# Mixer projections: halves of them moved between other TensorE steps, and half of the weights' low parts made by GpSimd

## The reference, cut to what matters

```python
h = _rmsnorm(x, norm1_g[l])            # 256 tokens, 1024 channels
p = h @ w_in[l]                        # 1024 x 4128
(gq, gk, gv, gz, ga, gb, mq, mk, mv, mo, mi, mf) = jnp.split(p, offsets, axis=-1)
y_a = _gdn_group(gq, gk, gv, gz, ga, gb, conv_w[l], ...)   # conv, silu, l2norm of q and k, gates
y_b = _mlstm_group(mq, mk, mv, mo, mi, mf, ...)
```

## Time and profile before

| | us |
|---|---|
| median of 3 runs | 1675.83 (1675.46 to 1678.76) |
| the profiled execution | 1690.07 |
| its span | 1688.2 |
| PE busy in the span | 1483.8 |
| DVE busy | 1105.5 |
| ACT busy | 583.5 |
| POOL busy | 828.1 |

### The profile page before, as it was taken

One profiled execution on the slowest core, in us unless ns is written; L12 is line 12 of the kernel. 1 busy time (PEld: TensorE's weight loads), 2 busy tenths in 40 slices (PEclk: granted clock), 3 DMA queues, 4 the chain that ended last, 5 costly groups with the idle time before them and its releaser, 6 DMA issues.

```text
span 1688.2 us, 22193 instructions
## 1 busy us (share of the span) xinstructions
PE 1483.8 (88%) x8310; PEld 1058.9 (63%) x8310; DVE 1105.5 (65%) x2162; ACT 583.5 (35%) x847; POOL 828.1 (49%) x746
## 2 busy tenths in 40 slices
PE   8999999756666799998878875889999989999999
PEld 7997675744222366665433431438998876699987
DVE  5865633797587868786756664317886547568865
ACT  6753331211121221232000001127665454466652
POOL 0025220467777765656667767642775113027750
PEclk9999999988787799999999987999999999999999
DMA  7447860698999999999999989995555554545451
GB/s 278 150 150 317 311 233 25 256 380 307 402 406 368 378 389 402 403 404 402 399 406 405 396 322 405 383 363 190 177 175 191 182 198 201 207 143 181 173 197 50
DMA packets 154251, 477.15 MB, mean 283 GB/s; under 512 B 10016, under 2 KB 12320, under 8 KB 150944
## 3 DMA queue, kind: packets, MB, share of 16 engines
q0 software_dynamic: 73728, 268.47, 41.1%
q1 hardware_dynamic: 80416, 207.27, 33.7%
HBM read 474.65 MB, written 1.05 MB: 282 GB/s over the span
## 4 chain that ended last, share of the span: by engine, by line
PE 56%; DVE 11%; DMA 11%; POOL 9%; issue 6%; ACT 2%; another core or an unknown queue 1%; ACTq 0%; DVEq 0%; POOLq 0%
PE ps L673 55%; POOL arena L2802 8%; DMA arena<-in_peer_v,cl 6%; DMA arena<-in_peer_u,arena 3%; DVE arena L1851 3%; PE ps L677 1%; POOL wring L2802 1%; DVE arena L1466 1%; DVE arena L1472 1%; DVE wring L1851 1%; DMA wring<-in_peer_u,arena 1%; DMA wring<-in_ada 1%; DVE st L2096 0%; DVE arena L1469 0%
## 5 line engine op out<-in xcount | busy, mean ns | idle before, releaser
L673 PE MATMUL ps<-arena,wring 128*128 128x256 f32 (+2 forms) x2360 | 603.4, 493 | 115.0 <-DMA arena<-in_peer_v,cl 92.2
L673 PEld LDWEIGHTS ps<-arena,wring 128*128 128x128 f32 (+1 forms) x2360 | 330.6, 167 | 368.6 <-issue 171.5
L1851 DVE CUSTOM_DVE_ANT_0 arena<-arena 128x1024 f32<-128x1024 f32 x214 | 257.2, 1225 | 141.4 <-DMA arena<-in_peer_u,arena 88.9
L2802 POOL DMA_INDIRECT arena<-in_peer_u,arena x214 | 243.0, 1136 | 201.7 <-DVE arena L1809 77.5
L2802 POOL DMA_INDIRECT arena<-in_peer_v,cl x214 | 231.0, 1080 | 85.5 <-issue 60.7
L673 PE MATMUL ps<-hhl,wh 128*128 128x256 f32 (+1 forms) x1056 | 252.4, 322 | 1.2 <-POOL hhl L2812 0.7
L2190 ACT ACT_TABLE_LOAD x64 | 82.1, 1283 | 406.5 <-DVE arena L1851 228.3
L1466 DVE TENSOR_TENSOR wl<-wring,wh 128x2048 fp32r<-128x2048 f32 (+1 forms) x76 | 168.1, 2212 | 60.0 <-ACT wh L2193 58.1
L673 PE MATMUL ps<-hhl,wl 128*128 128x256 f32 x704 | 198.5, 282 | 0.0
L673 PEld LDWEIGHTS ps<-hhl,wh 128*128 128x128 f32 x1056 | 175.6, 190 | 19.6 <-POOL hhl L2812 2.5
L2193 ACT ACTIVATE wh<-wring 128x2048 fp32r<-128x2048 f32 (+1 forms) x78 | 146.2, 1874 | 70.8 <-PE ps L673 69.0
(11 more groups left out here) (257 smaller groups left out, 2025.3 us busy)
## 6 DMA issues: line engine op xcount, KB each, us to landing
wring<-in_ups SPq DMA_DIRECT2D x33, 2048.0 KB
wring<-in_ada SPq DMA_DIRECT2D x24, 2048.0 KB, 11.5
wring<-in_ffn_w_down SPq DMA_DIRECT2D x12, 2048.0 KB
wring<-in_w_in SPq DMA_DIRECT2D x8, 2048.0 KB
wring<-in_ffn_w_down SPq DMA_DIRECT2D x6, 1536.0 KB
wring<-in_peer_wq SPq DMA_DIRECT2D x4, 2048.0 KB
wring<-in_attn_w_qkv SPq DMA_DIRECT2D x4, 2048.0 KB
wring<-in_w_out SPq DMA_DIRECT2D x2, 2048.0 KB
```

Of the source, the lines that this page charges most:

```text
L673: return pe.matmul(o, l, r, start=start, stop=stop)
L1851: ve.tensor_tensor_reduce(out=o, in0=o, in1=h2[:, t, :], scale=1.0, scalar=0.0, op0=MUL, op1=ADD, accum_out=dots[j % 2][:, k:k + 1]).then_ ...
L2802: po.indirect_dma_start(out=ring[n % NR], out_offset=None, in_=table, in_offset=bass.IndirectOffsetOnAxis(ap=which, axis=0)).then_inc(S[f" ...
```

## The change

Three things move. PE does the first half of projection 1 where six `busy` matmuls stood, ahead of `crow`, and the first half of projection 6 ahead of the l2 sums of q, whose five `busy` matmuls are taken out. The low parts of pieces 1, 3, 5, 7, 9 and 11 go from DVE to POOL, on a counter of their own, `g_wl`. And DVE's `lo_in(2)` stands ahead of the copy of `crow` instead of behind the negated maxima.

```diff
-        "v_gu": ("v_gps", 1), "v_ge": ("v_gu", 1), "v_gl": ("v_ge", 1), "v_wl": ("v_hT", 4), "a_wh": ("a_hTh", 1), "v_cum": ("v_gl", 1), "v_cc": ("v_cum", 1),
+        "g_lev": ("g_wl", 6), "v_gu": ("v_gps", 1), "v_ge": ("v_gu", 1), "v_gl": ("v_ge", 1), "v_wl": ("v_hT", 4), "a_wh": ("a_hTh", 1), "v_cum": ("v_gl", 1), "v_cc": ("v_cum", 1),
...
+    def low_there(p):
+
+        return ("g_wl", p // 2 + 1) if p % 2 == 1 and p < 12 else ("v_wl", p // 2 + 1 + p // 13)
...
-        def proj3(n):
+        def proj3(n, halves):
...
-            for g in range(2):
+            for g in halves:
                 b = take(("pj", 2 * n + g), "a_pj", 2 * n + g + 1)
                 for i in range(2):
                     p = 2 * n - 2 + (i if n == 3 else g)
-                    pe.wait_ge(*at("v_wl", p + 1))
+                    pe.wait_ge(*at(*low_there(p)))
...
         k.then_inc(S["p_cum"], 1)
-        busy(bank_ada[:, 0:128], 6)
+        proj(1, [0])
         pe.wait_ge(*at("v_cc", 1))
         b = take("crow", "v_crow", 1)
...
         def l2(g, n):
-            busy(bank_ada[:, 0:128], 5 * n)
             pe.wait_ge(*at("a_l2s", n + 1))
...
-        proj(1)
+        proj(1, [1])
         pe.wait_ge(*at("v_rows", 1))
...
         proj(5)
+        proj(6, [0])
         l2(0, 1)
         pe.wait_ge(*at("a_c16", 1))
         cond = conditioning(range(GROUPS_EARLY), sc32, "p_ada", 1)
-        proj(6)
+        proj(6, [1])
...
         def lo_in(n):
 
-            for p in range(2 * n - 2, 2 * n):
+            for p in (2 * n - 2, 2 * n - 1)[:1 + n // 7]:
                 ve.wait_ge(*at("a_wh", p + 1))
                 name, w, low = in_piece(p)
-                told(tt(low.bitcast(FR), w, wh_in[p % 4], SUB), "v_wl", p + 1)
+                told(tt(low.bitcast(FR), w, wh_in[p % 4], SUB), *low_there(p))
...
         seq(stt(NBE, EG, -1.0, bt, MUL, MUL))
+        lo_in(2)
         ve.wait_ge(*at("p_crow", 1))
...
-        lo_in(2)
         conv(1, 0)
...
+        for p in range(1, 12, 2):
+            po.wait_ge(*at("a_wh", p + 1))
+            name, w, low = in_piece(p)
+            told(po.tensor_tensor(low.bitcast(FR), w, wh_in[p % 4], SUB), *low_there(p))
         po.wait_ge(*at("d_l", 16))
         level(0)
```

More of the change, by code:

```diff
@@ L717, in _, with proj @@
         k.then_inc(S["p_g"], 1)
-        def proj(n):
+        def proj(n, halves=range(2)):
             if n > 0:
-                return proj3(n)
+                return proj3(n, halves)
             w = weights(("in", 0)).rearrange("p (k c) -> p k c", k=8)
```

## The result

The changed kernel takes 1689.26 us (median of 6 runs, 1687.56 to 1690.58), the kernel before 1676.53 us (6 runs, 1675.05 to 1679.16). The ratio is 1.0071 with a 95% interval of 1.0061 to 1.0081, so the change costs 12.7 us. The forecast was 1691.1 with a range of 1684.6 to 1694.4.

A forecast was written before the change was run, and what follows sets the result against it. PE, paced by the projections, was taken to bound the kernel, with DVE next. Projection 6 ending 13.6 us late plus 1.7 for the clock gave +15.3 on 1675.83: 1691.1 us, range 1684.6 to 1694.4.

The forecast's parts named there:

- Steps 1 and 2: Projection 1 and `crow`: POOL's low part of piece 3 holds DVE's scans until 44.5; PE waits 2.0 us, `em` at 46.3.
- the unseen case: DVE's scans beside POOL, which no row shows: taken as held until 44.5, so `v_rows` is there at 46.2.
- Steps 3 and 4: `conv(1, 0)` and `conv(2, 1)`: one POOL part holds each 4.5 us; k's l2 sums 5.3 later, decays 10.0 later.
- step 4: `conv(2, 1)`: POOL takes piece 7 in it, costing 4.5 us; decays at 81.7, 10.0 later, and PE waits for the reciprocal.
- step 7: Clock behind PE's waits: slack covers the earlier ones; behind the wait ahead of projection 6, half clock costs 1.7 us.
- Step 5: Second part of `conv(0, 2)`: starts at 107.4, held 4.5 us by piece 11; piece 9 meets only DVE work with PSUM input.
- Steps 6 and 7: Projection 6: PE waits 4.4 us for piece 10 and ends 13.6 us late; half clock behind the wait adds 1.7.
- (a): Rival at the convolutions: POOL gets its turn only after a run of convolution instructions; +11.8 us, 1687.6, chance 0.14.
- (b): Rival at the convolutions: multiply-adds of 256 columns are not held, so 4.15 us are gained; 1671.7, chance 0.10.
- Its price of 4.15 us: The most the change can bring PE: 1.43 and 1.2 us from `busy` matmuls, 1.52 from the wait at 75.68.
- (c): Rival for the whole kernel: something between, losses partly in slack; within 3.4 us of before, 1675, chance 0.05.

The follow-up runs named there:

- the fillers: The changed kernel with sixteen matmuls of ones put into PE's wait ahead of the first half of projection 6; ratio 1.0079 to the kernel before.

## Why the prediction was right

**Steps 1 and 2.** The first scan was held, 4.54 us against 0.68; this was the unseen case that I had to choose from its neighbours. `em` came at 45.93 (46.3 in the sum), behind a wait of 1.90 (2.0).

**Steps 3 and 4.** The l2 sums of k came at 62.02 (62.6), behind 4.13 us (4.4); the decays on DVE at 81.05 (81.7). A part inside a convolution costs 4.24, 4.38 and 4.22 us, not 4.5: of POOL's 4.72, 4.59 and 4.60 us, 0.2 to 0.5 overlap with DVE's work, not 0.1. One thing in step 4 was wrong: "4 to 5 us" of wait ahead of the transposes at 81.8 were 1.36. The granted clock was at 0.50 behind the wait of 4.13 us, from 62.0 to about 68.5, so that PE itself came later; the slack behind it ate that, as step 7 says.

**Step 5.** The second part of `conv(0, 2)` started at 106.72 (107.4). Piece 9 did meet DVE's own low part, which has two inputs in SBUF: 5.66 us instead of 4.6 on POOL. I had missed that; nobody waited for it.

**Steps 6 and 7.** The wait ahead of projection 6 was 4.28 us (4.4). The clock cost 2.5 us in the first profile, not 1.7: the 0.50 lasted beyond the 3.3 us that I had read behind the other wait. In the second profile it cost 1.6. Without the clock the stage would be 12.5 us late (13.6 in the sum), which the fillers show: 130.55 − 118.09; 0.3 of the 1.1 us between them was gone by the start of `conv(1, 0)`, 0.7 are the overlaps of the three parts, and 0.1 is the half. That the two errors cancel, 15.0 us against 15.3, is luck.

**Behind the stage.** The sum let the 15.3 us go through to the end. The medians have 12.7, and the second comparison of the same two kernels has a ratio of 1.0099, which is some 17 us. In the trace of the changed kernel 14.9 us are there up to 280 us, and as far as PE's mixer work goes none is given back. From 600 us on, where rows are gathered, executions differ among themselves by more than the 2.3 us that are missing (the two profiles of the changed kernel by 9 us at 1200 us). So whether the change gives anything back there stays open, and that the medians landed within 2.6 us of the forecast is in part luck.

**The rivals.** (a), in which POOL must wait for a whole convolution, is out: POOL's parts start inside it and take 4.6 to 4.8 us. (b), no hold on wide multiply-adds, is out by the 4.73 us. Its price of 4.15 us is not wholly out of reach, though: with GpSimd only writing, the stage gained 2.7 us of it. (c), within 3.4 us of before, is out by the 12.7.

## What to carry to other kernels

Before work is given to an idle GpSimd, look at what DVE does in the same microseconds, not at how busy it is. If DVE's instructions there have two inputs in SBUF, a GpSimd instruction that reads SBUF stopped DVE for nearly its whole length here, and 2.31 us saved cost 4.2. The same instruction beside DVE work with an input in PSUM cost nothing. So three more waits of GpSimd, which took its parts out of the convolutions, moved the stage from 15.0 us late to 0.6 us late. A wait of 4.28 us on PE cost 1.6 to 2.5 us more than itself, since no slack followed; count the clock behind such a wait.

## What I had not expected of the hardware

- A memset on GpSimd of 1.81 us leaves DVE's multiply-adds with two inputs in SBUF alone (16 in 8.30 us), but holds a negation with one input in SBUF: 1.73 us for 0.42.
- The granted clock can be low early without any wait beside it. With all low parts on DVE, the first half of projection 1 had 0.50, where it ran at 1.00 in the first profile of the changed kernel, and PE was busy without a gap from 28 us on before it:

```profile
32.40:35.60 3.20, 3.20 (x16) 3.20 (x16) 0.91 (x5) 1.47 (x2) 0.00 (x0) 0.50 1.02 387
```

Four of the twelve profiled executions had a clock of 0.50 to 0.70 in this stretch, one of them the kernel before. It costs 1.3 to 1.6 us at that place, which DVE's later waits mostly take up. What decides it I don't know.
